# Two output tiles side by side, in alternating banks, in the loops of a two-layer decoder step's MLP

## The chip, the cores and the metric

The kernel runs on one core of a Trainium2 chip. The metric is the device time of one execution in microseconds (us); smaller is better. TensorE does the matrix products, VectorE (DVE), ScalarE (ACT) and GpSimd (POOL) the elementwise work, SyncE (SP) issues transfers. PSUM is the memory that TensorE writes to; the kernel sees it as 8 banks of 128 partitions x 512 fp32 numbers.

## The reference

One inference step of a two-layer decoder trunk, for a prompt of 1024 tokens and a sample group of 8 sequences x 8 tokens, which share all weights. Layer 0 mixes by sliding-window attention and a gated short convolution, layer 1 by multi-scale pooling and dilated attention. Each layer then is

```
x = layer_norm(ALPHA * x + mixer(x))
x = layer_norm(ALPHA * x + square(relu(x @ w1)) @ w2)     # the MLP: w1 is 1024 x 4096, w2 is 4096 x 1024
```

all in fp32, with D_MODEL = 1024. The change is in the second line alone. The caches of keys and values are also copied to new outputs, shifted by the 8 new tokens.

## The kernel before

**Layout.** Activations are kept with features on the partitions: X is [128, 8, 1088], that is 8 chunks (KC) of 128 features by 1024 + 64 tokens. The tokens are worked in three groups (GROUP) of 384, 384 and 320 columns.

**Products in three passes.** Each fp32 operand is split into a high part of type fp32r and the rest, also fp32r: XS (or HID) holds both for the activations, WS both for the weights. For each chunk k of the contraction there are three matmuls, high x high, low weight x high and high weight x low, all into the same bank. `product` (L1187 to L1195) writes such a unit: 3 x 8 = 24 matmuls of 128x128 weights by 384 (or 320) columns for an input product, 3 x 4 = 12 for a down product. Every matmul has a weight load of its own.

**The MLP.** The hidden width of 4096 is cut into N_HB = 8 blocks of 512. For each block the *hidden* stage (`hidden_super`) makes 12 units: for each group g, 4 tiles j of 128 hidden features, from weight tile j. The *down* stage (`down_super`) makes 24 units: for each group, 8 output tiles m, two (mm) from each of 4 weight tiles. The first hidden stage and the last down stage of a layer also carry the layer norm's transposes between their units (`weave` is not None, `ln_weave`); what lies between runs in a hardware loop of N_HB - 1 = 7 rounds per layer, each one down stage and one hidden stage, with `weave` None. TensorE's instructions run in program order, and so do those of each other engine; semaphores tie them together.

**Banks.** Hidden unit u writes bank 4 + u % 2, down unit v bank 6 + v % 2. Before a unit TensorE waits until the unit two before it has been taken out of the bank: `h_evac` (L1378 to L1380) or `p_evac` (L1396).

**Behind a hidden unit.** ScalarE waits for h_mm and makes Relu from the bank to RT (L621), Square to ST (L625), Copy to HID's high part (L627), then issues one part of the caches' copy (L641); VectorE subtracts to get HID's rest (L976, hid_ready). In the last group it then casts a weight tile of the down stage (L798, `w_high_loop`).

**Behind a down unit.** VectorE adds the bank to X (L995). In the last group it casts a tile of the next hidden stage after every second unit (L798).

**Weight tiles.** A tile is 128 x 1024. SyncE loads it into one of NRAW = 2 buffers WR (L316) as soon as the tile two before has been split; VectorE casts it to the high part in one of NSLOT = 4 slots of WS; GpSimd makes the rest (L458) and counts w_split, for which TensorE waits in group 0 of a stage. The cast stands in VectorE's program behind the work on the unit that last used that slot, and no semaphore other than that order guards the slot.

Of the kernel before, what the change touches and what calls it, by code (L numbers as in the profile page):

```python
# [12 lines left out]
P = 128  # L13
# [3 lines left out]
KC = D_MODEL // P  # L17
# [15 lines left out]
GROUP = ((0, 384), (384, 384), (768, 320))  # L33
# [11 lines left out]
NSLOT = 4  # L45
# [16 lines left out]
U_MLP = (U_EOUT + 3 * EVEN_OUT, U_EOUT + 3 * EVEN_OUT + N_HB * 24 + 3 * ODD_IN + 12 + 3 * ODD_OUT)  # L62
# [21 lines left out]
def build(nc, io):  # L84
    F32, F32R = mybir.dt.float32, mybir.dt.float32r
    ALU, ACT, AX = mybir.AluOpType, mybir.ActivationFunctionType, mybir.AxisListType
    ctx = ExitStack()
    with ctx:
        place = [nc.sbuf_base + (-nc.sbuf_base) % 64]

        def at(name, shape, dtype, offset):
            return nc.alloc_sbuf_tensor_at(name, shape, dtype, offset=offset)
# [17 lines left out]
        X = at("X", [P, KC, NT], F32, o_xr)  # L110
        XS = at("XS", [P, 2, KC, NT], F32R, o_xs)
        HID = at("HID", [P, 2, 4, NT], F32R, o_hr)
        Y = at("Y", [P, KC, NT], F32, o_hr)
        WS = at("WS", [P, NSLOT, 2, 1024], F32R, o_ws)
# [3 lines left out]
        RT = at("RT", [P, 2, 384], F32, o_scr + 12288)  # L118
# [77 lines left out]
        def bank(b, n=512):  # L196
            return PS[:, b, 0:n]

        def sem(name):
            return ctx.enter_context(nc.semaphore(name))  # L200
# [9 lines left out]
        p_mm, p_evac = sem("p_mm"), sem("p_evac")  # L210
        h_mm, h_evac, h_sq, hid_hi, hid_ready = sem("h_mm"), sem("h_evac"), sem("h_sq"), sem("hid_hi"), sem("hid_ready")
# [17 lines left out]
        def back_bank(l, g, k):  # L229

            return (2, 3, 6, 7)[k % 4] if (l, g) == (3, 2) else 2 + k % 2

        def rows_out(l, g):

            return ZE if (l, g) == (3, 2) else ZN
# [41 lines left out]
        def parts_d(m):  # L277

            n = 2 * (step_d(m)[1] + 1)
            return [(i, min(4, n - i)) for i in range(0, n, 4)]  # L280
# [6 lines left out]
        for m in range(STEPS_D + 2):  # L287
            b, phase = divmod(m, PER_SEQ)
# [214 lines left out]
        def _(act):  # L503
# [110 lines left out]
            def hidden_super(l, i, weave, copy):  # L614

                for g, (c0, gw) in enumerate(GROUP):
                    for j in range(4):
                        u = 4 * g + j
                        n = 12 * i + (H_UNITS * l + u)
                        act.wait_ge(h_mm, n + 1)  # L620
                        act.activation(RT[:, u % 2, 0:gw], bank(4 + u % 2, gw), ACT.Relu).then_inc(h_evac, 1)  # L621
                        act.wait_ge(h_evac, n + 1)
                        if not (isinstance(n, int) and n < 2):
                            act.wait_ge(hid_ready, n - 1)
                        act.activation(ST[:, u % 2, 0:gw], RT[:, u % 2, 0:gw], ACT.Square).then_inc(h_sq, 1)  # L625
                        act.wait_ge(h_sq, n + 1)
                        act.activation(HID[:, 0, j, c0:c0 + gw], ST[:, u % 2, 0:gw], ACT.Copy).then_inc(hid_hi, 1)  # L627
                        cache_copy(*copy, u)
                        if weave is not None and g < 2:
                            ln_weave(weave, 3 + g, j)  # L630

            def cache_copy(name, out, b, part):

                n = (D_WINDOW - DEC_SEQ) // COPY_PARTS
                if isinstance(b, int):
                    src, dst = io[name][b:b + 1], io[out][b:b + 1]
                else:
                    src, dst = io[name][bass.ds(b, 1)], io[out][bass.ds(b, 1)]
                src = src[:, DEC_SEQ + n * part:DEC_SEQ + n * (part + 1), :].rearrange("a s f -> a (s f)")
                dst = dst[:, n * part:n * (part + 1), :].rearrange("a s f -> a (s f)")  # L640
                act.dma_start(dst.rearrange("a (k f) -> (a k) f", k=16),  # L641
                              src.rearrange("a (k f) -> (a k) f", k=16)).then_inc(copied, 16)
# [90 lines left out]
            for m in range(STEPS_D):  # L733
                b, phase = divmod(m, PER_SEQ)
                n = len(parts_d(m))
# [32 lines left out]
        def _(dve):  # L768
# [26 lines left out]
            def w_high_loop(i, t):  # L795

                dve.wait_ge(w_in[t % NRAW], 64 * i + 16 * (t // NRAW + 1))
                dve.tensor_copy(WS[:, t % NSLOT, 0, :], WR[:, t % NRAW, :]).then_inc(w_hi, 1)  # L798
# [24 lines left out]
            def taken(u):  # L823
                return bank(6 + u % 2)
# [96 lines left out]
            for s in range(4):  # L921
                for g in range(3):
                    for j in range(4):
                        u = 12 * s + 4 * g + j
# [18 lines left out]
            for g in range(3):  # L943
                for j in range(2):
                    u = 48 + 2 * g + j
# [40 lines left out]
            def down_super(l, i, weave, first=False):  # L986
                for g, (c0, gw) in enumerate(GROUP):
                    for m in range(8):
                        v = 8 * g + m
                        dve.wait_ge(p_mm, 24 * i + (U_MLP[l] + v + 1))  # L990
                        if first:
                            dve.scalar_tensor_tensor(out=X[:, m, c0:c0 + gw], in0=X[:, m, c0:c0 + gw], scalar=ALPHA,  # L992
                                                     in1=taken(v)[:, 0:gw], op0=ALU.mult, op1=ALU.add).then_inc(p_evac, 1)
                        else:
                            dve.tensor_tensor(X[:, m, c0:c0 + gw], X[:, m, c0:c0 + gw], taken(v)[:, 0:gw],  # L995
                                              ALU.add).then_inc(p_evac, 1)
                        if g == 2 and m % 2 == 1:
                            if weave is None:
                                w_high_loop(i, T_MLP[l] + m // 2 + 2 * NSLOT)
                            elif l == 0:  # L1000
                                w_high(T_OIN + m // 2)
                        if weave is not None and m % 2 == 1:
                            ln_weave(weave, g, m // 2)
# [151 lines left out]
            for m in range(STEPS_D):  # L1155
                b, phase = divmod(m, PER_SEQ)
# [21 lines left out]
            c0, gw = GROUP[2]  # L1178
# [7 lines left out]
        def _(pe):  # L1186
            def product(out, slot, off, nk, src, g, done):  # L1187
# [7 lines left out]
                        n += 1  # L1195
                last.then_inc(done, 1)

            def unit(u, t, g):

                if g == 0:  # L1200
                    pe.wait_ge(w_split, t + 1)
                if u >= 2:
                    pe.wait_ge(p_evac, u - 1)
                product(bank(6 + u % 2), t % NSLOT, 0, KC, XS, g, p_mm)
# [161 lines left out]
            def hidden_super(l, i, weave, done):  # L1366

                t0 = T_MLP[l]
                for g in range(3):
                    if weave is not None:  # L1370
                        pe.wait_ge(x_split, XS_LN[2 * l] + 8 * (g + 1))
                        if g == 0:
                            pe.wait_ge(zn_ready, 18 * l + 5)
                    for j in range(4):
                        u = 4 * g + j
                        n = 12 * i + (H_UNITS * l + u)
                        if g == 0:
                            pe.wait_ge(w_split, 8 * i + (t0 + j + 1))  # L1378
                        if not (isinstance(n, int) and n < 2):
                            pe.wait_ge(h_evac, n - 1)  # L1380
                        product(bank(4 + u % 2), (t0 + j) % NSLOT, 0, KC, XS, g, h_mm)
                        if weave is not None and g < 2:
                            ln_weave(weave, 3 + g, j, done)

            def down_super(l, i, weave):

                t0 = T_MLP[l] + 4
                done = [U_MLP[l] + 24 * (N_HB - 1) + 8 * g + 8 for g in range(3)]
                for g in range(3):
                    pe.wait_ge(hid_ready, 12 * i + (H_UNITS * l + 4 * g + 4))  # L1390
                    for j in range(4):
                        if g == 0:
                            pe.wait_ge(w_split, 8 * i + (t0 + j + 1))
                        for mm in range(2):
                            v = 8 * g + 2 * j + mm
                            pe.wait_ge(p_evac, 24 * i + (U_MLP[l] + v - 1))  # L1396
                            product(bank(6 + v % 2), (t0 + j) % NSLOT, 4 * mm, 4, HID, g, p_mm)
                        if weave is not None:
                            ln_weave(weave, g, j, done)
                return done  # L1400
# [8 lines left out]
            done = mlp(0, out_projection(0, T_EOUT, U_EOUT, XS_MIX0))  # L1409
# [10 lines left out]
            for s in range(4):  # L1420
                for g in range(3):
                    if s == 0:
                        pe.wait_ge(x_split, XS_LN1 + 8 * (g + 1))
                    for j in range(4):
                        n = 4 * g + j
# [12 lines left out]
                if s == 2:  # L1438
# [3 lines left out]
                    for c in range(4):  # L1442
                        last = pe.transpose(PS[0:NS, 3, c * P:c * P + P], KTD[:, c, SEQ:NT], IDN[:, :])
# [97 lines left out]
            for m in range(STEPS_D):  # L1541
                b, phase = divmod(m, PER_SEQ)
                n = len(parts_d(m))
# [22 lines left out]
            done = mlp(1, out_projection(1, T_OOUT, U_OOUT, XS_MIX1))  # L1566
# [152 lines left out]
```

## Time and profile before

| what | us |
|---|---|
| median of 3 runs | 2589.13 |
| lowest and highest | 2588.72, 2597.13 |
| the profiled execution's own time | 2585.44 |
| its span, first to last instruction | 2583.4 |
| TensorE busy with matmuls in the span | 2462.0 |
| VectorE, ScalarE, GpSimd busy | 915.0, 627.0, 504.9 |

A profile is of one execution. Its groups name the source line, the engine, the operation and the tiles written and read; a group's busy time is the union of its instructions on the engine, so for overlapping matmuls it is less than count x mean: one matmul is in flight for 334 ns, while the next starts long before that. The step from one matmul to the next therefore has to be read from starts, not from the mean of one.

### The profile page before, as it was taken

How to read it: one execution, taken by the hardware profiler on the slowest of the kernel's cores; microseconds unless marked ns; L12 is line 12 of the kernel's file. 1: busy time of each engine (PE TensorE's matmuls, PEld its weight loads, DVE VectorE, ACT ScalarE, POOL GpSimd, SP SyncE). 2: the span in 40 equal slices, each digit the busy share in tenths (PEclk: the TensorE clock that was granted, in tenths of full speed). 3: DMA queues.
4: the chain of work that ended last, by engine and by line, in shares of the span. 5: the costliest groups of instructions: out<-in, count | busy, mean ns of one | idle time of the engine just before them, and what ended most of it. 6: DMA issues, size and time to landing. Idle time of an engine off the chain costs nothing.

```text
span 2583.4 us, 39454 instructions
## 1 busy us (share of the span) xinstructions
PE 2462.0 (95%) x16054; PEld 2344.8 (91%) x16054; DVE 915.0 (35%) x2028; ACT 627.0 (24%) x1352; POOL 504.9 (20%) x254
## 2 busy tenths in 40 slices
PE   6999998999999999998999798898999999999996
PEld 6988997999999999998998455798999999999995
DVE  3455534222322322327135445434322322322325
ACT  1223305121121022023101556505121121122122
POOL 2111214221211211213220000114221211211210
PEclk9999999999999999999999899999999999999998
DMA  5200412232232232222111956402232232232221
GB/s 161 72 22 32 119 33 66 74 122 65 81 113 70 84 105 76 92 92 82 54 58 59 274 191 250 143 33 66 78 118 70 80 109 76 87 97 81 87 76 70
DMA packets 77253, 240.12 MB, mean 93 GB/s; under 512 B 25168, under 2 KB 42192, under 8 KB 69328
## 3 DMA queue, kind: packets, MB, share of 16 engines
q1 hardware_dynamic: 60464, 167.65, 19.4%
q10 hardware_dynamic: 16688, 71.05, 9.5%
q8 instruction: 73, 1.20, 0.2%
q14 instruction: 28, 0.23, 0.0%
HBM read 224.78 MB, written 81.71 MB: 119 GB/s over the span
## 4 chain that ended last, share of the span: by engine, by line
PE 80%; issue 7%; DVE 6%; ACT 3%; POOL 2%; DMA 1%; SPq 1%; POOLq 0%; DVEq 0%; ACTq 0%
PE PS L1193 70%; POOL WS L458 2%; PE PS L1222 1%; PE PS L1471 1%; PE PS L1457 1%; DVE ZN L820 1%; PE PS L1483 1%; PE PS L1496 1%; PE PS L1522 1%; PE PS L1271 1%; PE PS L1238 1%; DMA KC<-in_kt 1%; DVE XS L785 1%; ACT X L539 1%; DMA WR<-in_w 1%
## 5 line engine op out<-in xcount | busy, mean ns | idle before, releaser
L1193 PE MATMUL PS<-XS,WS 128*128 128x384 f32 (+1 forms) x8208 | 1382.9, 328 | 33.8 <-DVE XS L785 19.5
L1193 PEld LDWEIGHTS PS<-XS,WS 128*128 128x128 f32 x8208 | 1355.5, 189 | 48.5 <-issue 36.1
L458 POOL TENSOR_TENSOR WS<-WR,WS 128x1024 fp32r<-128x1024 f32 x178 | 436.1, 2450 | 1900.2 <-DVE WS L798 1059.9
L1193 PE MATMUL PS<-HID,WS 128*128 128x384 f32 (+1 forms) x4608 | 765.4, 326 | 2.2 <-DVE X L995 2.1
L1193 PEld LDWEIGHTS PS<-HID,WS 128*128 128x128 f32 x4608 | 758.3, 188 | 4.6 <-DVE X L995 4.3
L621 ACT ACTIVATE RT<-PS 128x384 f32<-128x384 f32 (+1 forms) x192 | 91.0, 474 | 1113.3 <-PE PS L1193 1113.3
L976 DVE TENSOR_TENSOR HID<-ST,HID 128x384 fp32r<-128x384 f32 (+1 forms) x192 | 105.8, 551 | 632.2 <-ACT HID L627 632.2
L995 DVE TENSOR_TENSOR X<-X,PS 128x384 f32<-128x384 f32 (+1 forms) x336 | 177.5, 531 | 401.3 <-PE PS L1193 401.1
L625 ACT ACTIVATE ST<-RT 128x384 f32<-128x384 f32 (+1 forms) x192 | 97.5, 508 | 7.8
L627 ACT ACTIVATE HID<-ST 128x384 fp32r<-128x384 f32 (+1 forms) x192 | 97.5, 508 | 6.1
L471 POOL TENSOR_TENSOR XS<-X,XS 128x384 fp32r<-128x384 f32 (+1 forms) x72 | 69.0, 967 | 91.7 <-ACT XS L543 88.1
L798 DVE CAST WS<-WR 128x1024 fp32r<-128x1024 f32 x112 | 77.0, 688 | 9.7 <-DMA WR<-in_w 9.2
L539 ACT ACTIVATE X<-PS,COLS 128x384 f32<-128x384 f32 (+1 forms) x92 | 59.0, 647 | 56.8 <-PE PS L1222 55.9
L548 ACT ACTIVATE SD<-VE 128x1 f32<-128x1 f32 (+1 forms) x36 | 7.3, 203 | 255.9 <-DVE VE L810 255.9
L962 DVE TENSOR_TENSOR X<-X,PS 128x384 f32<-128x384 f32 (+1 forms) x48 | 25.3, 529 | 114.6 <-PE PS L1193 114.3
L1222 PE MATMUL PS<-IDN,ZN 128*128 128x128 f32 (+1 forms) x264 | 44.5, 288 | 21.7 <-ACT X L539 13.2
L1222 PEld LDWEIGHTS PS<-IDN,ZN 128*128 128x128 f32 (+1 forms) x264 | 31.0, 144 | 34.7 <-ACT X L539 19.2
L793 DVE CAST WS<-WR 128x1024 fp32r<-128x1024 f32 x66 | 49.5, 751 | 12.5 <-DMA WR<-in_w 12.3
L820 DVE TENSOR_SCALAR ZN<-PS,MV,RS 128x1024 f32<-128x1024 f32 (+1 forms) x33 | 44.3, 1343 | 10.9 <-PE PS L1222 9.9
L992 DVE SCALAR_TENSOR_TENSOR X<-X,PS 128x384 f32<-128x384 f32 (+1 forms) x48 | 25.5, 531 | 60.7 <-PE PS L1193 60.7
L1457 PE MATMUL PS<-KTD,Y 64*128 64x512 f32 (+3 forms) x192 | 43.6, 554 | 1.6 <-DVE MNA L1110 0.7
L1471 PEld LDWEIGHTS PS<-IDN,SMB 128*128 128x128 f32 x208 | 26.3, 160 | 18.1 <-DVE SMB L1122 10.6
(166 smaller groups left out, 1220.4 us busy)
## 6 DMA issues: line engine op xcount, KB each, us to landing
WR<-in_w SPq DMA_DIRECT2D x178, 512.0 KB, 3.3
out_d_ks<-in_cache_d_k ACTq DMA_DIRECT2D x96, 340.0 KB
out_d_vs<-in_cache_d_v ACTq DMA_DIRECT2D x96, 340.0 KB
KC<-in_kt SPq DMA_DIRECT2D x16, 1024.0 KB, 9.7
VCD<-in_cache_d_v SPq DMA_DIRECT2D x16, 1024.0 KB, 7.2
TH<-in_th SPq DMA_DIRECT2D x4, 1024.0 KB, 8.2
KC<-in_kt SPq DMA_DIRECT2D x8, 512.0 KB, 6.5
VCD<-in_cache_d_v SPq DMA_DIRECT2D x32, 128.0 KB, 7.4
```

What stands on the lines that cost most here:

```text
L458: pool.tensor_tensor(WS[:, slot, 1, :], WR[:, raw, :], WS[:, slot, 0, :].bitcast(F32), ALU.subtract).then_inc(w_split, 1)
L539: act.activation(X[:, k, c0:c0 + gw], bank(back_bank(l, g, k), gw), ACT.Identity, scale=col(C_LNG + KC * l + k), bias=col(C_LNB + KC * l + ...
L621: act.activation(RT[:, u % 2, 0:gw], bank(4 + u % 2, gw), ACT.Relu).then_inc(h_evac, 1)
L625: act.activation(ST[:, u % 2, 0:gw], RT[:, u % 2, 0:gw], ACT.Square).then_inc(h_sq, 1)
L627: act.activation(HID[:, 0, j, c0:c0 + gw], ST[:, u % 2, 0:gw], ACT.Copy).then_inc(hid_hi, 1)
L798: dve.tensor_copy(WS[:, t % NSLOT, 0, :], WR[:, t % NRAW, :]).then_inc(w_hi, 1)
L820: dve.tensor_scalar(rows_out(l, g)[0:r, tt, :], FT[0:r, :], MV[0:r, 0:1], RS[0:r, 0:1], ALU.subtract, ALU.mult).then_inc(zn_ready, 1)
L976: dve.tensor_tensor(HID[:, 1, j, c0:c0 + gw], ST[:, u % 2, 0:gw], HID[:, 0, j, c0:c0 + gw].bitcast(F32), ALU.subtract).then_inc(hid_ready, 1)
L995: dve.tensor_tensor(X[:, m, c0:c0 + gw], X[:, m, c0:c0 + gw], taken(v)[:, 0:gw], ALU.add).then_inc(p_evac, 1)
L1193: last = pe.matmul(out[:, 0:gw], WS[:, slot, a, (off + k) * P:(off + k + 1) * P], src[:, b, k, c0:c0 + gw], start=(n == 0), stop=(n == 3 * ...
L1222: last = pe.transpose(PS[:, back_bank(l, g, k), tt * P:tt * P + r], rows_out(l, g)[0:r, tt, k * P:k * P + P], IDN[0:r, 0:r])
L1457: last = pe.matmul(bank(2 * (u % 2) + h, nk * P), Y[rows, 4 + c, qb * P:qb * P + P], KTD[rows, c, k * P:(k + nk) * P], start=True, stop=True)
```

## The change

In the loops alone (`weave` None), two units are issued together: `pair` goes through the 24 (hidden) or 12 (down) steps, and at each makes one matmul for the first output tile and one for the second, in two banks. A hidden pair is units u - 1 and u, of two weight tiles; a down pair is the two output tiles v and v + 1 of one weight tile. Four banks serve each kind: hidden pairs take 4, 5 and 0, 1 by turns, down pairs 6, 7 and 2, 3. A pair waits once, until the pair before the last is out of its banks. The counters h_mm and p_mm are raised at the last matmul of each tile, which are now the last two of a pair. The readers on ScalarE and VectorE look into the new banks, in the same order as before; the woven stages are as they were.

```diff
+        def hidden_bank(u, paired):
+            return (4, 5, 0, 1)[u % 4] if paired else 4 + u % 2
+        def down_bank(v, paired):
+            return (6, 7, 2, 3)[v % 4] if paired else 6 + v % 2
...
-                        act.activation(RT[:, u % 2, 0:gw], bank(4 + u % 2, gw), ACT.Relu).then_inc(h_evac, 1)
+                        act.activation(RT[:, u % 2, 0:gw], bank(hidden_bank(u, weave is None), gw), ACT.Relu).then_inc(h_evac, 1)
...
-                            dve.tensor_tensor(X[:, m, c0:c0 + gw], X[:, m, c0:c0 + gw], taken(v)[:, 0:gw],
+                            dve.tensor_tensor(X[:, m, c0:c0 + gw], X[:, m, c0:c0 + gw], bank(down_bank(v, weave is None), gw),
                                               ALU.add).then_inc(p_evac, 1)
...
+            def pair(outs, weights, nk, src, g, done):
+                c0, gw = GROUP[g]
+                n = 0
+                for k in range(nk):
+                    for a, b in ((0, 0), (1, 0), (0, 1)):
+                        for out, (slot, off) in zip(outs, weights):
+                            last = pe.matmul(out[:, 0:gw], WS[:, slot, a, (off + k) * P:(off + k + 1) * P],
+                                             src[:, b, k, c0:c0 + gw], start=(n == 0), stop=(n == 3 * nk - 1))
+                            if n == 3 * nk - 1:
+                                last.then_inc(done, 1)
+                        n += 1
...
+                        if weave is None:
+                            if j % 2:
+                                pe.wait_ge(h_evac, n - 1 if u == 1 else n - 3)
+                                pair((bank(hidden_bank(u - 1, True)), bank(hidden_bank(u, True))),
+                                     (((t0 + j - 1) % NSLOT, 0), ((t0 + j) % NSLOT, 0)), KC, XS, g, h_mm)
+                            continue
...
+                        if weave is None:
+                            v = 8 * g + 2 * j
+                            pe.wait_ge(p_evac, 24 * i + (U_MLP[l] + (v if v == 0 else v - 2)))
+                            pair((bank(down_bank(v, True)), bank(down_bank(v + 1, True))),
+                                 (((t0 + j) % NSLOT, 0), ((t0 + j) % NSLOT, 4)), 4, HID, g, p_mm)
+                            continue
```

TensorE at the start of a down stage in the loop, before (REGISTER_ALU and ISA rows compute or make a wait against a counter of the loop):

```order
L1393 ISA [waits hid_ready]
L1396 ISA [waits w_split]
L1193 MATMUL PS<-HID,WS 128x384 [waits p_evac]
L1193 MATMUL PS<-HID,WS 128x384 x11
L1396 REGISTER_ALU
L1193 MATMUL PS<-HID,WS 128x384 [waits p_evac]
L1193 MATMUL PS<-HID,WS 128x384 x11
L1393 REGISTER_ALU
L1396 REGISTER_ALU [waits w_split]
```

and of the changed kernel at the same place:

```order
L1420 ISA [waits hid_ready]
L1423 ISA [waits w_split]
L1213 MATMUL PS<-HID,WS 128x384 [waits p_evac]
L1213 MATMUL PS<-HID,WS 128x384 x23
L1420 REGISTER_ALU
L1213 MATMUL PS<-HID,WS 128x384 [waits p_evac,w_split]
L1213 MATMUL PS<-HID,WS 128x384 x23
```

Two runs of 12 matmuls, each behind a wait for its bank, have become one run of 24 behind one wait. The waits for weight tiles stand where they stood, one for every 24 matmuls.

TensorE at the start of a hidden stage in the loop, before:

```order
L1378 ISA
L1380 ISA [waits w_split]
L1193 MATMUL PS<-XS,WS 128x384 [waits h_evac]
L1193 MATMUL PS<-XS,WS 128x384 x23
L1378 REGISTER_ALU
L1193 MATMUL PS<-XS,WS 128x384 [waits h_evac,w_split]
L1193 MATMUL PS<-XS,WS 128x384 x23
```

and of the changed kernel:

```order
L1399 ISA
L1399 REGISTER_ALU [waits w_split]
L1402 REGISTER_ALU [waits w_split]
L1213 MATMUL PS<-XS,WS 128x384 [waits h_evac]
L1213 MATMUL PS<-XS,WS 128x384 x47
```

Here the wait for the second weight tile has moved ahead of the first unit's matmuls: the stage starts when two tiles are split, and 48 matmuls follow one wait.

## Rows read from the trace of the kernel before

**Rows 1.** The page: busy us of TensorE, its granted clock in tenths, the two dearest matmul groups.

```profile
PE 2462.0 (95%) x16054; PEld 2344.8 (91%) x16054; DVE 915.0 (35%) x2028; ACT 627.0 (24%) x1352; POOL 504.9 (20%) x254
...
PEclk9999999999999999999999899999999999999998
...
L1193 PE MATMUL PS<-XS,WS 128*128 128x384 f32 (+1 forms) x8208 | 1382.9, 328 | 33.8 <-DVE XS L785 19.5
...
L1193 PE MATMUL PS<-HID,WS 128*128 128x384 f32 (+1 forms) x4608 | 765.4, 326 | 2.2 <-DVE X L995 2.1
```

**Rows 2.** Stretches (from:to, us, busy by engine, clock): both loops, a down half, a hidden half.

```profile
472.01:1135.33 663.32, 663.19 (x4029) 662.41 (x4028) 170.52 (x308) 125.21 (x252) 134.48 (x56) 1.00 0.28 88
1827.00:2490.00 663.00, 662.97 (x4027) 662.15 (x4026) 168.96 (x308) 125.18 (x252) 133.64 (x56) 1.00 0.27 88
...
899.24:946.62 47.38, 47.38 (x291) 47.38 (x289) 8.94 (x16) 16.51 (x33) 7.98 (x5) 1.00 0.36 114
851.69:899.24 47.55, 47.55 (x291) 47.34 (x289) 15.23 (x28) 1.38 (x3) 11.23 (x5) 1.00 0.19 62
```

**Rows 3.** Timeline of TensorE: start, us to the last end, group [idle before, releaser].

```profile
851.69 47.71 PE L1193 MATMUL PS<-HID,WS 128*128 128x384 f32 x288
899.24 47.54 PE L1193 MATMUL PS<-XS,WS 128*128 128x384 f32 x288
```

**Rows 4.** Timeline of ScalarE, the Relus of units that follow each other.

```profile
907.78 0.49 ACT L621 ACTIVATE RT<-PS 128x384 f32<-128x384 f32 x1 [2.47 <-PE PS L1193]
...
911.94 0.49 ACT L621 ACTIVATE RT<-PS 128x384 f32<-128x384 f32 x1 [2.55 <-PE PS L1193]
...
936.26 0.44 ACT L621 ACTIVATE RT<-PS 128x320 f32<-128x320 f32 x1 [1.91 <-PE PS L1193]
...
939.78 0.44 ACT L621 ACTIVATE RT<-PS 128x320 f32<-128x320 f32 x1 [2.08 <-PE PS L1193]
```

**Rows 5.** Timeline of TensorE, two matmuls each: within a unit, across units, at a stage's start.

```profile
908.63 0.51 PE L1193 MATMUL PS<-XS,WS 128*128 128x384 f32 x2
...
907.41 0.51 PE L1193 MATMUL PS<-XS,WS 128*128 128x384 f32 x2
...
899.41 0.52 PE L1193 MATMUL PS<-XS,WS 128*128 128x384 f32 x2
```

**Rows 6.** Timeline of VectorE, the evacuations of two down units that follow each other.

```profile
858.33 0.56 DVE L995 TENSOR_TENSOR X<-X,PS 128x384 f32<-128x384 f32 x1 [1.69 <-PE PS L1193]
860.40 0.55 DVE L995 TENSOR_TENSOR X<-X,PS 128x384 f32<-128x384 f32 x1 [1.52 <-PE PS L1193]
```

**Rows 7.** Timeline of TensorE: first down matmuls of each loop and behind each loop.

```profile
472.01 0.51 PE L1193 MATMUL PS<-HID,WS 128*128 128x384 f32 x2
...
1136.14 0.51 PE L1193 MATMUL PS<-HID,WS 128*128 128x384 f32 x2
...
1826.80 3.48 PE L1193 MATMUL PS<-HID,WS 128*128 128x384 f32 x19
...
2490.88 1.40 PE L1193 MATMUL PS<-HID,WS 128*128 128x384 f32 x7
```

**Rows 8.** Timeline around the longest wait for a bank, 658 to 668 us.

```profile
657.55 2.41 POOL L458 TENSOR_TENSOR WS<-WR,WS 128x1024 fp32r<-128x1024 f32 x1 [1.11 <-DVE WS L798]
...
663.67 3.52 PE L1193 MATMUL PS<-HID,WS 128*128 128x384 f32 x17
...
665.01 0.69 DVE L798 CAST WS<-WR 128x1024 fp32r<-128x1024 f32 x1 [0.91 <-DMA WR<-in_w]
665.62 1.06 DVE L995 TENSOR_TENSOR X<-X,PS 128x384 f32<-128x384 f32 x2
```

**Rows 9.** Timeline behind the second unit of a hidden stage's last group.

```profile
844.85 0.44 ACT L621 ACTIVATE RT<-PS 128x320 f32<-128x320 f32 x1 [2.08 <-PE PS L1193]
...
846.33 0.49 DVE L976 TENSOR_TENSOR HID<-ST,HID 128x320 fp32r<-128x320 f32 x1 [2.43 <-ACT HID L627]
...
846.73 0.69 DVE L798 CAST WS<-WR 128x1024 fp32r<-128x1024 f32 x1
847.50 2.41 POOL L458 TENSOR_TENSOR WS<-WR,WS 128x1024 fp32r<-128x1024 f32 x1 [1.11 <-DVE WS L798]
```

More of the change, by code:

```diff
@@ L992, in down_super @@
                             dve.scalar_tensor_tensor(out=X[:, m, c0:c0 + gw], in0=X[:, m, c0:c0 + gw], scalar=ALPHA,
-                                                     in1=taken(v)[:, 0:gw], op0=ALU.mult, op1=ALU.add).then_inc(p_evac, 1)
+                                                     in1=bank(down_bank(v, weave is None), gw), op0=ALU.mult, op1=ALU.add).then_inc(p_evac, 1)
                         else:
-                            dve.tensor_tensor(X[:, m, c0:c0 + gw], X[:, m, c0:c0 + gw], taken(v)[:, 0:gw],
+                            dve.tensor_tensor(X[:, m, c0:c0 + gw], X[:, m, c0:c0 + gw], bank(down_bank(v, weave is None), gw),
                                               ALU.add).then_inc(p_evac, 1)
```

## The prediction

> **What bounds the kernel now.** I read the page first. Its busy table gives TensorE 2462.0 of 2583.4 us at a granted clock of nine tenths or more nearly everywhere, and the dearest groups are the three-pass products of L1193 [rows 1]. So the question is not which engine bounds the MLP's loops, but whether TensorE waits in them or what one of its steps costs. The table by stretches answers the first half: over the two loops TensorE is busy 663.19 of 663.32 us and 662.97 of 663.00 us, at a clock of 1.00 (the 2.4 GHz level), while VectorE has 170 us of work, ScalarE 125, GpSimd 134 [rows 2]. In the timeline one hidden half of 288 products starts at 899.24 and the next down half at 946.62, 47.38 us later; the down half before it began at 851.69 and took 47.55 [rows 2, 3].
>
> The second half is the step. Successive Relus of a hidden stage start 4.16 us apart for 384 columns and 3.52 us apart for 320 [rows 4]; a unit is 24 matmuls, so a step is 173.3 ns and 146.7 ns. The 64 columns between them cost 26.7 ns, 0.417 ns each (one column per cycle at 2.4 GHz). So 384 columns stream for 160.0 ns and every step carries a fixed 13.3 ns that does not depend on the columns. Check: 192 x 173.3 + 96 x 146.7 = 47.36 us, against 47.38 measured. The hidden half has nothing in it but steps.
>
> **The change part by part.** The loops make 2 layers x 7 rounds x 576 = 8064 of the matmuls. Their number, sizes and weight loads stay; only their order does not.
>
> *Banks alternate at every matmul.* In the kernel before, the bank changes once per unit. The trace has that case: two matmuls within a unit (908.63 on) fill 0.51 us from the first start to the last end; the last of one unit and the first of the next, which writes the other bank (907.41 on), fill 0.51 us too [rows 5]. The unit's own period says it more finely: 23 steps inside at 173.3 ns leave 4.16 - 3.986 = 0.174 us for the one that changes banks. Down units: 2.07 us for 12 steps, 172.5 ns within the rounding, with a bank change twice as often and no dearer [rows 6]. So a bank change is neither gain nor loss, and I take 0 for it. What the rows do not show is a matmul that adds to a bank other than the one just written; the first of a unit overwrites. Bounds: at best the whole 13.3 ns goes, 8064 x 13.3 ns = 107 us; at worst each step becomes like the longest step without a wait, 12 ns more (two matmuls in 0.52 us rather than 0.51; I read the extra as 5 to 15 ns) [rows 5], 8064 x 12 ns = 97 us. Both ends are far; the nearest row is the bank change itself, at zero.
>
> *Fewer waits for a free bank.* The pair waits for banks that were left a whole pair earlier. In the loops this replaces waits that are nearly all over already. What they cost now is measured from loop start to loop end: 472.01 to 1136.14 is 664.13 us, 1826.80 to 2490.88 is 664.08 us [rows 7]; fourteen rounds without a stall would be 14 x 2 x 47.38 = 1326.64 (a down half has the same columns and steps), so 1.57 us are lost in all. Where: just behind a hidden stage VectorE has to cast the fourth weight tile, whose transfer is late (idle 0.91 us on the DMA), and the first evacuation of the down stage stands behind it in VectorE's program; TensorE's third unit waits for that bank. In the worst case 17 matmuls take 3.52 us where 16 x 173.3 + 334 ns = 3.11 was due, 0.41 us lost [rows 8]. With four banks the third unit needs no old bank; the evacuation is first needed by the third pair, 8.3 us into the stage. The stall goes: 1.57 us gained.
>
> *Later evacuation of the even unit.* Both units of a pair end together, so the even one is taken 4.16 us later in a hidden stage (2.08 in a down stage). ScalarE needs 1.48 us from a Relu's start to the end of HID's Copy [rows 9], twice that and two transfer issues, 3 to 3.6 us, per pair of 7.0 to 8.3 us; VectorE 1.1 us (two of 0.55 [rows 6]) per down pair of 4.2: hidden.
>
> *Weight tiles.* These follow the evacuations. Take the down stage that starts at 851.69 [rows 3]. The four units of the 320-column group ahead of it end 3.52 us apart [rows 4], the second at 844.85 and the fourth at 851.89; after, they end as pairs at these two times. The rows show what follows a unit that ends at 844.85: its Relu then, VectorE's rest at 846.33, the cast at 846.73, GpSimd's rest at 847.50 for 2.41 us [rows 9]. So down tile 0 takes exactly the time that tile 1 has now: ready at 849.91, needed at 851.69, 1.8 us to spare. Tile 1 is cast meanwhile and leaves GpSimd at 849.91 + 2.4 = 852.3; the second down pair needs it one pair of 4.16 us in, at 855.85. Tile 2 may be loaded from 849.91; the longest time from release to cast is 665.01 - (657.55 + 2.41) = 5.05 us [rows 8], so cast at 854.96, ready 858.1, needed at 860.0: 1.9 to spare. Tile 3: loaded from 852.3, cast 857.4, ready 860.6, needed at 864.2. VectorE takes pair 0 of the down stage behind that cast, 858.0 to 859.1; pair 2 wants the banks at 860.0: 0.9 us to spare, the smallest margin of all. The other way round (tiles of the next hidden stage, cast in the down stage's last group) the cast moves by one evacuation, 0.49 us. A hidden pair needs both its tiles at its start: tiles 0 and 1 at once, 2 and 3 8.3 us later. Down pairs of 320 columns end 3.52 us apart, the last at the stage's start; two evacuations, the cast of 0.69 and GpSimd's 2.41 us end some 4.1 us behind a pair. So tile 1 is ready 7.04 - 4.1 = 2.9 us before the stage begins and tile 3 4.1 us after. Hidden, at no cost.
>
> The Trainium skill, trace analysis page (Perfetto Trace Analysis, section "Matmul Optimizations"), asks that all 8 PSUM banks be used for more parallelism; by that rule this change should pay. The trace bounds what it can be worth here at the 1.57 us above, since TensorE has no other wait in the loops. The page TensorE: Matmul & The Clock Gate (section "Back-to-back issue gap") gives a warm gap of N/2.4 + 2.5 ns, against the fixed 13.3 ns here. By it some 10.8 ns of each step would be avoidable, an estimate of 87 us if the alternation avoided it; its gap is for an isolated stream, and this trace has no step as short.
>
> **Sum.** Profiled execution: span 2583.4 - 1.6 = 2581.8, its time 2585.44 - 1.6 = 2583.9. The median of the three runs is 3.7 us above the profiled one; the forecast keeps that: 2589.13 - 1.6 = 2587.5 us, rounded.
>
> **The rivals.** (A) The fixed 13.3 ns is a wait of an accumulation on its own bank, and alternation hides it. For it: it is independent of the column count, and back-to-back adds to one bank is what the change breaks up. Against: the step that changes banks is as long. 2589.1 - 107 - 2 = 2480 us; half of it, 2534. 5%.
> (B) Slower: the weight transfer at the hidden-to-down seam. Now ScalarE issues its cache copies a unit apart (3.52 us); after, two within 2 us right behind each pair, just where tiles 2 and 3 are loaded. Place: the cast of tile 3 holds VectorE, pair 2 of the down stage waits. It begins to cost when release to cast passes 5.05 + 0.9 = 6.0 us; it makes the kernel over 0.3% slower once 14 seams cost (7.8 + 1.6) / 14 = 0.67 us each, thus from 6.7 us on; at double the longest now seen, 10.1 us, it costs 14 x 4.1 = 57 us, 2645 us. For it: the longest is 5.05 us already, and it made VectorE idle [rows 8]. Against: that much more has no row. 5%.
> (C) Adding to the other bank costs a little, as bounded above: up to 97 us, 2685; over 0.3% from (7.8 + 1.6) us / 8064 = 1.2 ns a step. Against: the same row as for A. 3%.
> (D) The change doesn't do what it says: were the pairs reordered back or serialised, the time would be 2587 to 2589 as well; no separate chance.
>
> **How the numbers follow.** 0.3% is 7.8 us, about what a measurement of this kernel tells from no change. My forecast (step unchanged, stall gone, nothing else late) has 87%, and its own spread is that of the runs before, 2588.72 to 2597.13, and of a few us of seams: 2580 to 2597, all within the 0.3% but for the last 2%. Faster 0.07 (A and 2 for its weaker forms and the runs' scatter), slower 0.09 (B, C and scatter), same 0.84. The rivals' times are so far off and so rare that the range leaves them out: 2578 to 2598.
>
> **What would show it.** Right: hidden halves of 47.38 us, down halves all 47.38 and none longer, Relus in twos, 8.32 us apart, the step 173.3 ns, the two loops 663.3 us each, the cast of down tile 0 some 3.5 us later. Wrong: any step other than 173 ns in the pairs (A or C), TensorE waiting on the cast or on X's evacuation 8 us into a down stage (B), a wait for w_split at the first pair.

## The result, and the profile after

The change makes the kernel a little slower. Over 12 runs each its median is 2596.74 us (2592.64 to 2601.79) against 2589.07 us (2583.07 to 2597.85); the ratio is 1.0025, 95% interval 1.0014 to 1.0036, that is 3.6 to 9.3 us more. The forecast was 2587.5 us and no change that a measurement can tell. One of the 11 executions of the kernel before that the first four experiments stand beside took 6184.87 us; every ratio is of the other, fast ones.

The first thing to look at is what the forecast rested on: the loops. The timeline of TensorE in the changed kernel (start, us to the last end, group, count) and a stretch of 200 us (from:to, us, busy us of TensorE, its weight loads, VectorE, ScalarE, GpSimd, then the granted clock):

```profile
573.44 47.54 PE L1213 MATMUL PS<-HID,WS 128*128 128x384 f32 x288
620.82 0.51 PE L1213 MATMUL PS<-XS,WS 128*128 128x384 f32 x2
```

```profile
600.00:800.00 200.00, 200.00 (x1218) 200.00 (x1218) 53.03 (x93) 35.75 (x72) 38.77 (x16) 1.00 0.27 84
```

A down half lasts from 573.44 to 620.82, 47.38 us, what a half without a stall took before [rows 2, 3]; of the 28 halves in the two loops' 14 rounds, 25 read 47.38 and the others 47.41. TensorE is busy without a gap, and the Relus of a hidden stage come in twos, 8.32 us apart. So alternation costs and gives nothing per step, and the 1.57 us of small stalls [rows 7] are all but gone. Both parts came out as forecast. The page shows where something did change:

```profile
L984 DVE TENSOR_TENSOR HID<-ST,HID 128x384 fp32r<-128x384 f32 (+1 forms) x192 | 145.7, 759 | 631.5 <-ACT HID L635 631.2
...
L1201 PE MATMUL PS<-HID,WS 128*128 128x384 f32 (+1 forms) x576 | 101.7, 335 | 8.3 <-DVE X L1003 8.3
```

The second row is the woven down stages, the ones behind the loops, which the change did not touch: TensorE idles 8.3 us before them, waiting for VectorE's addition to X. Before, all the down stages together had 2.2 us of that [rows 1]. The first row says that VectorE's subtraction for HID's rest now takes 759 ns in the mean; the page of the kernel before has 551 ns for it (its L976): 25 of the 192 take over 1 us, where 2 did.

The timeline at the first of the two places, behind the loop of layer 0, unfolds it:

```profile
1137.70 2.40 POOL L466 TENSOR_TENSOR WS<-WR,WS 128x1024 fp32r<-128x1024 f32 x1 [39.02 <-DVE WS L806]
...
1138.34 2.11 DVE L984 TENSOR_TENSOR HID<-ST,HID 128x320 fp32r<-128x320 f32 x1 [0.72 <-ACT HID L635]
...
1142.04 4.35 PE L1201 MATMUL PS<-HID,WS 128*128 128x384 f32 x24
...
1144.52 0.69 DVE L806 CAST WS<-WR 128x1024 fp32r<-128x1024 f32 x1 [0.46 <-DMA WR<-in_w]
...
1145.29 2.36 POOL L466 TENSOR_TENSOR WS<-WR,WS 128x1024 fp32r<-128x1024 f32 x1 [1.76 <-DVE WS L806]
1145.42 2.58 DVE L984 TENSOR_TENSOR HID<-ST,HID 128x320 fp32r<-128x320 f32 x1 [0.20 <-ACT HID L635]
1148.07 0.69 DVE L806 CAST WS<-WR 128x1024 fp32r<-128x1024 f32 x1
1148.67 1.01 DVE L1003 TENSOR_TENSOR X<-X,PS 128x384 f32<-128x384 f32 x2
...
1149.37 6.84 PE L1201 MATMUL PS<-HID,WS 128*128 128x384 f32 x29 [2.98 <-DVE X L1003]
```

TensorE makes two units (24 matmuls) from 1142.04 and then wants bank 6 back for the third. VectorE is still at the work of the last hidden pair: a subtraction that takes 2.58 us because GpSimd's split runs beside it, the fourth cast, and only then the addition that frees the bank. The third unit starts at 1149.37 instead of 1146.22, 3.15 us late; at the second place it is 3.41 us, and there it is the load of the fourth tile that comes last: VectorE was idle for 0.86 us, until its transfer had landed, ahead of the cast at 2508.17. And it does not end there. The stretch behind the wait:

```profile
1151.00:1154.00 3.00, 3.00 (x11) 3.00 (x10) 0.55 (x1) 0.00 (x0) 0.22 (x1) 0.50 0.50 175
```

The granted clock is 0.50, the 1.2 GHz level, after TensorE had stood still for 3 us; eleven matmuls are in flight in 3 us, a step of 320 ns. Summed over the steps that are too long, about ten at each place, this adds 1.6 us at each. The account: 2 x (3.3 + 1.6) = 9.8 us lost, 1.6 us gained, 8.2 us, against 7.7 us between the medians.

The profiled execution of the changed kernel has a span of 2599.8 us, 16.4 us over before, not 8.2. The other 8 us lie outside: its first loop alone starts at 478.68 against 472.01 [rows 7]. Nothing was changed ahead of that loop. The clock differs there: in the changed kernel's trace it is 0.50 in the stretches 270.5 to 273.3, 410.5 to 413.3, 444.5 to 447.3 and 454.8 to 457.6 us, and 1.00 at the same places of the trace before. The kernel with four banks and no pairs, below, whose time is that of before, has the clock at 0.50 in the same four stretches and its first loop at 478.55. So these 6.7 us don't come with the change; why one execution loses the clock there and another doesn't is open.

### The profile page after: what moved, and what is told of

Same layout as the page of the kernel before. It is cut to its first block, busy times and chain, and to the rows that moved or that the text cites. A ratio compares the mean times of both kernels' runs of the same rounds, so it can differ in the third digit from the quotient of the medians.

```text
span 2599.8 us, 39202 instructions
## 1 busy us (share of the span) xinstructions
PE 2470.7 (95%) x16054; PEld 2354.9 (91%) x16054; DVE 939.9 (36%) x2028; ACT 627.0 (24%) x1352; POOL 505.7 (19%) x254
## 4 chain that ended last, share of the span: by engine, by line
PE 87%; DVE 6%; ACT 3%; DMA 1%; SPq 1%; issue 1%; POOL 1%; ACTq 0%; DVEq 0%
PE PS L1213 50%; PE PS L1201 27%; PE PS L1243 1%; PE PS L1504 1%; PE PS L1490 1%; DVE ZN L828 1%; PE PS L1516 1%; DMA WR<-in_w 1%; PE PS L1529 1%; PE PS L1259 1%; PE PS L1555 1%; PE PS L1292 1%; DMA KC<-in_kt 1%; DVE XS L793 1%; ACT X L547 1%
## 5 line engine op out<-in xcount | busy, mean ns | idle before, releaser
L984 DVE TENSOR_TENSOR HID<-ST,HID 128x384 fp32r<-128x384 f32 (+1 forms) x192 | 145.7, 759 | 631.5 <-ACT HID L635 631.2
L1003 DVE TENSOR_TENSOR X<-X,PS 128x384 f32<-128x384 f32 (+1 forms) x336 | 164.6, 528 | 378.3 <-PE PS L1213 335.9
L970 DVE TENSOR_TENSOR X<-X,PS 128x384 f32<-128x384 f32 (+1 forms) x48 | 25.4, 530 | 114.6 <-PE PS L1201 114.3
L1243 PEld LDWEIGHTS PS<-IDN,ZN 128*128 128x128 f32 (+1 forms) x264 | 31.5, 145 | 34.9 <-ACT X L547 19.5
```

What stands on the lines that cost most here:

```text
L984: dve.tensor_tensor(HID[:, 1, j, c0:c0 + gw], ST[:, u % 2, 0:gw], HID[:, 0, j, c0:c0 + gw].bitcast(F32), ALU.subtract).then_inc(hid_ready, 1)
L1243: last = pe.transpose(PS[:, back_bank(l, g, k), tt * P:tt * P + r], rows_out(l, g)[0:r, tt, k * P:k * P + P], IDN[0:r, 0:r])
```

## The experiments

### Four banks in the woven down stage

```diff
-            return (6, 7, 2, 3)[v % 4] if paired else 6 + v % 2
+            return (6, 7, 2, 3)[v % 4] if paired or v < 8 else 6 + v % 2
...
-                            pe.wait_ge(p_evac, 24 * i + (U_MLP[l] + v - 1))
-                            product(bank(6 + v % 2), (t0 + j) % NSLOT, 4 * mm, 4, HID, g, p_mm)
+                            pe.wait_ge(p_evac, 24 * i + (U_MLP[l] + (v - 3 if v < 8 else v - 1)))
+                            product(bank(down_bank(v, False)), (t0 + j) % NSLOT, 4 * mm, 4, HID, g, p_mm)
```

> The changed kernel, and in the last down stage of each layer (the one outside the loop, which follows a paired hidden stage) the first token group's eight units use banks 6, 7, 2, 3 in turn and wait for the bank four units back. Theory 1 (seam): the loss is TensorE's wait for bank 6 at the third unit of that stage, 3.15 and 3.4 us in the profile, and the half-clock steps behind it, some 1.4 us each: 2 x 4.7 = 9.4 us come back, so 2596.7 - 9.4 = 2587.3 us, ratio to before 0.9993. Rival 2 (step): the alternation of banks costs something spread over the loops, which this edit leaves: 2596 us. Rival 3 (drift ahead of the loops, 6.7 us later at the first loop in the one profile): 2590 to 2596 us, with the profile's first loop again starting some us later than at 472 us.

Measured: 2586.16 us, beside 2589.36 for the kernel before on the same chip; ratio 0.9988 (0.9973 to 1.0002). The whole loss is gone with two places of the program edited. The step is out as the cause, and so is a drift of the size that rival 3 needs (2590 us at least; the interval ends at 2589.9). The timeline of TensorE at the place, now without a gap:

```profile
1138.12 8.16 PE L1201 MATMUL PS<-HID,WS 128*128 128x384 f32 x46
```

46 matmuls in 8.16 us, (8.16 - 0.33) / 45 = 174 ns a step. VectorE is as late as in the changed kernel (its first addition starts 6.82 us into the stage, there 6.63); the third unit no longer asks. By the two ratios, 1.0014 at least and 1.0002 at most, this version beats the changed kernel, though the two were not run side by side; against the kernel before, the interval just holds no change.

### Only the down stages paired

The changed kernel without the branch for pairs in `hidden_super`, and with `bank(4 + u % 2, gw)` in ScalarE's Relu.

> Only the down stages of the loops are paired (banks 6, 7, 2, 3); hidden units are made one by one in banks 4, 5 as before. Theory 1 (seam): the wait needs a paired hidden stage ahead of a two-bank down stage, and there is none, so the time is that of before less the 1.6 us of small stalls in the loops: 2587.5 us; third unit of the woven down stage waits at most 0.4 us. Rival 2 (step): down pairs are a third of a hidden and down round's... half of the loops' matmuls, so half of the loss stays: 2593 us.

Measured: 2585.26 us; ratio 0.9987 (0.9968 to 1.0005). With alternating banks in half of the loops' matmuls nothing is lost: it is the hidden pairs that bring the wait. One point of the expectation missed: at the second place the third unit waits 0.66 us, not 0.4 at most (0.00 at the first). There VectorE was idle for 1.37 us ahead of the fourth cast, until the load had landed: the small stall of the kernel before, with a later load.

### Only the hidden stages paired

The changed kernel without the branch for pairs in `down_super`, and with `taken(v)` in VectorE's additions.

> Only the hidden stages of the loops are paired; all down stages, in the loops too, are made unit by unit in two banks. Theory 1 (seam): now each of the 14 paired hidden stages is followed by a two-bank down stage, whose third unit waits some 3.2 us for bank 6 and then runs about 1.4 us longer at half the clock: 14 x 4.6 = 64 us over before, 2653 us; without the clock's part 2634 us. The down halves in the loops read 50.6 to 52 us. Rival 2 (step): 2593 us, nothing special at the seams.

Measured: 2662.42 us; ratio 1.0282 (1.0263 to 1.0301), 73 us over before. Now every paired hidden stage has a two-bank down stage behind it, and the cost repeats: in its profile there are 14 waits of 2.9 to 3.7 us at these seams, one of 1.06 us at the first down stage of layer 0 (whose hidden stage is not paired), together 46.9 us, and 27.2 us of steps that are too long behind them, 74.1 in all. The forecast was 9 us short: the long steps cost 1.4 to 2.9 us at a seam, not 1.4, and the down halves behind a paired hidden stage take 51.8 to 53.7 us. One seam in the timeline:

```profile
670.37 4.35 PE L1201 MATMUL PS<-HID,WS 128*128 128x384 f32 x24
...
673.08 2.38 POOL L466 TENSOR_TENSOR WS<-WR,WS 128x1024 fp32r<-128x1024 f32 x1 [1.21 <-DVE WS L806]
...
673.72 2.08 DVE L984 TENSOR_TENSOR HID<-ST,HID 128x320 fp32r<-128x320 f32 x1 [0.72 <-ACT HID L635]
676.77 0.69 DVE L806 CAST WS<-WR 128x1024 fp32r<-128x1024 f32 x1 [0.97 <-DMA WR<-in_w]
677.38 1.01 DVE L1003 TENSOR_TENSOR X<-X,PS 128x384 f32<-128x384 f32 x2
```

Nearly the same picture: 2.08 us of subtraction until just behind GpSimd's end, then 0.97 us for the load of the tile, then the cast, then the bank.

### Four banks, no pairs

```diff
-                            if j % 2:
-                                pe.wait_ge(h_evac, n - 1 if u == 1 else n - 3)
-                                pair(...)
+                            pe.wait_ge(h_evac, n - u if u < 4 else n - 3)
+                            product(bank(hidden_bank(u, True)), (t0 + j) % NSLOT, 0, KC, XS, g, h_mm)
                             continue
...
+                            for mm in range(2):
+                                v = 8 * g + 2 * j + mm
+                                pe.wait_ge(p_evac, 24 * i + (U_MLP[l] + (0 if v < 4 else v - 3)))
+                                product(bank(down_bank(v, True)), (t0 + j) % NSLOT, 4 * mm, 4, HID, g, p_mm)
```

> The loops' units use the four banks in turn, as in the changed kernel, but are made one after the other, no pairs. Theory 1 (seam): evacuations and casts keep the pace of before, so no seam wait; the four banks remove the small stalls of the loops: 2587.5 us, down halves all 47.38 us. Rival 2 (the new banks themselves, 0 to 3, cost something, wherever): 2593 to 2597 us.

Measured: 2587.97 us; ratio 0.9997 (0.9982 to 1.0012), and down halves in the loops of 47.38 us. The interval ends at 2592.5 us, below rival 2: the banks themselves are neutral. The small stalls go, but 1.6 us is below what these runs resolve.

### What makes VectorE so late: four edits on the kernel with hidden pairs only

That kernel shows the seam 14 times, so a part of a wait can be measured there.

(a) Square in PSUM, so that the subtraction reads one tile of SBUF instead of two:

```diff
+                        sq = bank(2 + u % 2, gw) if weave is None else ST[:, u % 2, 0:gw]
-                        act.activation(ST[:, u % 2, 0:gw], RT[:, u % 2, 0:gw], ACT.Square).then_inc(h_sq, 1)
+                        act.activation(sq, RT[:, u % 2, 0:gw], ACT.Square).then_inc(h_sq, 1)
```

and `sq` as the source of HID's Copy and of VectorE's subtraction.

> As the kernel with hidden pairs only (2662 us, seam waits of 2.9 to 3.7 us, mean 3.3), but in the loops ScalarE puts the Square into the free banks 2 and 3 of PSUM instead of ST, so VectorE's subtraction for HID's rest has one operand in SBUF instead of two. Theory A (shared port): that subtraction takes 2.1 to 2.6 us where it meets GpSimd's split only because both read two tiles in SBUF; now none of the loops' takes over 0.7 us. The second cast then starts some 1.5 us earlier, the tile's split ends 1.0 us earlier (behind GpSimd's first), and with it the load and the fourth cast: waits 3.3 - 1.0 = 2.3 us, 14 of them, 14 us less, 2648 us. Rival B (GpSimd slows any VectorE instruction, whatever its operands): subtractions and waits stay, 2662 us.

(b) GpSimd splits 512 of a tile's 1024 columns in the loops and leaves the rest of the other 512 uncomputed:

```diff
-                pool.tensor_tensor(WS[:, slot, 1, :], WR[:, raw, :], WS[:, slot, 0, :].bitcast(F32),
+                pool.tensor_tensor(WS[:, slot, 1, 0:w], WR[:, raw, 0:w], WS[:, slot, 0, 0:w].bitcast(F32),
```

> As the kernel with hidden pairs only, but in the loops GpSimd splits the first 512 of a weight tile's 1024 columns and leaves the rest part of the others as it was (part of the computation is left out). GpSimd's instruction takes 1.2 us instead of 2.4. Theory A (the chain cast, split, load, cast, evacuation sets the wait, and the subtraction is held by the split): held subtractions end 1.2 us sooner, loads are released 1.2 to 2.2 us sooner, waits 1.5 to 1.8 us instead of 3.3; 2662 - 14 x 1.7 = 2638 us, less if the clock then stays up. Rival B (the wait is TensorE's for something else than VectorE's evacuation): 3.3 us stay.

(c) Half of each tile is loaded in the loops; the other half keeps old numbers:

```diff
-                sp.dma_start(WR[:, (t0 + j) % NRAW, :],
-                             io["w"][bass.ds(t, 1), :, :].rearrange("a p n -> (a p) n")).then_inc(w_in[(t0 + j) % NRAW], 16)
+                sp.dma_start(WR[:, (t0 + j) % NRAW, 0:512],
+                             io["w"][bass.ds(t, 1), :, 0:512].rearrange("a p n -> (a p) n")).then_inc(w_in[(t0 + j) % NRAW], 16)
```

> As the kernel with hidden pairs only, but the loops load only the first 512 columns of each weight tile (the others keep old numbers; part of the computation is left out). From a tile's release to its cast then takes some 3 us instead of 4.5. Theory A (fourth cast waits for both, the held subtraction and the load, about equally late): the subtraction still ends at 5.6 to 5.9 us into the stage, so the waits shrink only by 0.3 to 0.6 us, to 2.8: 2655 us. Rival C (the load alone sets it): waits 3.3 - 1.5 = 1.8 us, 2641 us.

(d) Both (a) and (c).

> Both edits: the Square in PSUM and half weight loads, on the kernel with hidden pairs only. Theory A: neither the subtraction nor the load holds the fourth cast; it starts about 4.0 us into the stage and the first evacuation ends at 5.1: waits of 1.1 us, what the pairs' late end alone costs, since ScalarE's second unit and VectorE's work for it only end 3.9 us into the stage. 2662 - 14 x 2.2 = 2631 us, and to 2606 us if a wait this short leaves the clock up. Rival C: as with half loads alone.

Measured, with the waits for the bank and the excess of the steps that are too long behind them, each summed over the 16 down stages of one profile; the usual wait is the median of the down stages behind a hidden pair:

| kernel | us | ratio to before | waits, us: sum, usual one | long steps, us |
|---|---|---|---|---|
| hidden pairs only | 2662.42 | 1.0282 (1.0263 to 1.0301) | 46.9, 3.3 | 27.2 |
| (a) Square in PSUM | 2634.58 | 1.0169 (1.0126 to 1.0213) | 34.9, 2.3 (1.9 to 3.3) | 12.1 |
| (b) half split | 2615.22 | 1.0098 (1.0064 to 1.0133) | 22.6, 1.27 | 4.3 |
| (c) half load | 2643.80 | 1.0198 (1.0171 to 1.0226) | 35.6, 2.37 | 21.1 |
| (d) (a) and (c) | 2612.36 | 1.0090 (1.0061 to 1.0120) | 28.4, 1.89 | 1.4 |

The first row was measured beside a kernel before of 2589.36 us, the others on another chip beside one of 2591.25 us. The two last columns account for the time over before to within 9 us. The two down stages behind the loops have waits of 2.3 to 3.7 us in all four; their own weight tiles are loaded and split outside the loop, in full in (b) and (c) too.

(a) The time is 28 us less rather than 14 (four runs, 2623 to 2645 us), because the waits were followed by the half clock less often (12.1 us against 27.2). VectorE's rows on its page:

```profile
L985 DVE TENSOR_TENSOR HID<-PS,HID 128x384 fp32r<-128x384 f32 (+1 forms) x168 | 89.9, 535 | 560.1 <-ACT HID L636 559.7
...
L807 DVE CAST WS<-WR 128x1024 fp32r<-128x1024 f32 x112 | 100.9, 901 | 20.1 <-DMA WR<-in_w 20.1
```

The subtraction takes 535 ns in the mean, against 784 with two operands in SBUF; of 192 one takes over 1 us, against 28, and that one is of a stage with ST. So it is not GpSimd's work as such that holds the subtraction, but where its operands lie. But the hold did not go away, it moved to the cast: 901 ns in the mean against 687, and 23 of the 112 over 1 us, where none was. The second cast at a seam now begins beside GpSimd's first split and is held until behind its end (1.94 us from 670.09, where the split ends at 671.47), so the second split starts only 0.4 us earlier, counted from the first, and not 1.0 as theory A had it. That the usual wait came out at A's 2.3 us is in part luck; the single waits lie between 1.9 and 3.3, and in the longest VectorE was idle for 2.52 us ahead of the fourth cast, until the load had landed.

(b) saved more than expected: the wait is 1.27 us rather than 1.5 to 1.8, and behind it the clock stayed up. Half of the 47 us saved is waits, half is the clock. It shortens the hold and releases the loads earlier at once, and doesn't say which counts for how much.

(c) fell between A's 2.8 and C's 1.8. The fourth cast no longer waits for the load but follows the held subtraction at once, and is 1 us earlier for it: both set the fourth cast, neither alone.

(d) missed: 1.89 instead of 1.1 us. Its timeline shows why:

```profile
669.32 2.37 POOL L466 TENSOR_TENSOR WS<-WR,WS 128x1024 fp32r<-128x1024 f32 x1 [1.59 <-DVE WS L807]
...
669.94 0.49 DVE L985 TENSOR_TENSOR HID<-PS,HID 128x320 fp32r<-128x320 f32 x1 [0.70 <-ACT HID L636]
670.70 1.54 DVE L807 CAST WS<-WR 128x1024 fp32r<-128x1024 f32 x1 [0.27 <-DMA WR<-in_w]
672.16 1.00 DVE L1004 TENSOR_TENSOR X<-X,PS 128x384 f32<-128x384 f32 x2
```

The subtraction is free (0.49 us beside GpSimd), and the cast, SBUF to SBUF, meets GpSimd's split: 1.54 us instead of 0.69. I had counted it at 0.69. Its long steps, 1.4 us in all, are one step of 0.1 us too much behind each wait; the clock never left the 2.4 GHz level at a seam.

## Why the prediction was wrong

- *Step unchanged*: right. 47.38 us per half in the changed kernel, and per down half and hidden half in each variant where nothing is waited for; rivals A and C did not occur.
- *Small stalls removed*: right in kind; 1.5 of the 1.57 us went.
- *Weight tiles hidden in the loops*: right. No wait for w_split or for a bank in the loops, although the margin of 0.9 us for pair 2 was worked out without a held subtraction: the second unit's takes 2.1 us where it meets the split, not 0.49.
- *Later evacuation of the even unit* and *Weight tiles*, put at "hidden" and "at no cost" for the seams behind the loops too: this is the step that failed. The working asked who waits for VectorE in the down stage that follows, and answered with four banks: "the evacuation is first needed by the third pair, 8.3 us into the stage". That holds for the paired down stages. The last hidden stage of each loop is paired too, and the down stage behind it is the woven one, with two banks, where the third unit needs the first evacuation 4.17 us in. The prediction's own numbers already price it: VectorE done with pair 0's first addition at 858.6 by the worst load, needed at 851.69 + 4.17 = 855.86, so 2.7 us twice. The front matter's "the woven stages are as they were" was true of their code and not of what reaches them.
- *Its size*: 3.15 and 3.41 us rather than 2.7, although the loads took 4.4 and 4.8 us from release to cast and not the 5.05 reckoned: a held subtraction stands in the chain. The trace of before had the sign of it, which the prediction doesn't mention:

```profile
661.36 2.40 POOL L458 TENSOR_TENSOR WS<-WR,WS 128x1024 fp32r<-128x1024 f32 x1 [1.41 <-DVE WS L798]
663.42 0.69 DVE L976 TENSOR_TENSOR HID<-ST,HID 128x320 fp32r<-128x320 f32 x1 [2.13 <-ACT HID L627]
```

  The subtraction ends 0.35 us behind GpSimd's end of 663.76. Before, the casts came a unit apart and the subtraction nearly always missed the split (7 of 192 took over 0.6 us); two units at once put the second unit's subtraction right onto the first tile's split.
- *The clock* has no term in the prediction. Its fall behind each wait cost 1.6 us. With it the seams cost 2 x (3.3 + 1.6) = 9.8 us where the prediction had nothing.
- Rival B had the right place in VectorE's program (the fourth cast, the seam) but the wrong partner: it looked for 14 seams with a slow load, and gave 5%. It was two seams, and no load slower than the 5.05 us seen before was needed.
- The signs that were to show the forecast right came true, for they were all of the loops, where it is right. And the measured 2596.74 us lies in the range of 2578 to 2598 by luck: the range was made for the scatter of runs and a few us of seams, not for this loss.

## What to carry to other kernels

When a stage in a loop is given more buffers, list every consumer and follower of it, and above all the peeled first and last stages: they keep the old depth but get the new rhythm. Finishing two tiles together saves nothing for a TensorE that is always busy and bunches everything behind it; the work of the second tile then overlaps what the first one set off, here GpSimd's split. Where the engine that is waited for is VectorE, check which of its instructions overlap GpSimd's, and where their operands lie.

## What the runs showed of the hardware

- A VectorE subtraction with both operands in SBUF, started while GpSimd works on SBUF tiles, ends some 0.35 us behind GpSimd's instruction, whatever is left of it (2.11 us from 1138.34, GpSimd's end 1140.10; 2.58 us from 1145.42, its end 1147.65; alone 0.49). In the changed kernel all 25 that started with over 0.3 us of GpSimd's work left did so. With one operand in PSUM it takes 0.49 us beside GpSimd, 24 times of 24 in (a) and 27 of 27 in (d). A cast from SBUF to SBUF is held in the same way, and ends some 0.55 us behind GpSimd's instruction (1.54 or 1.94 us instead of 0.69); the additions to X, one operand in PSUM, are not held (0.55 us each). In all of these GpSimd had started first; for the other order nothing is shown here.
- The Trainium skill, page SBUF — State Buffer, section "Who interferes with whom", says so: a VectorE instruction with two SBUF inputs contends with a GpSimd instruction that reads SBUF, and a cast can run in a two-port mode that contends too; the shared ports go to the one that issues first for its whole instruction, and the other blocks fully. The numbers above agree; in which mode the cast ran, no run here shows.
- By that rule a held subtraction could have been priced before the run, from rows of the kernel before; this is an estimate. The first tile's split starts 1.17 us behind the first unit's subtraction (847.50 - 846.33) and takes 2.41 [rows 9]; the second unit's subtraction comes 1.5 to 1.8 us behind the first (the prediction's 3 to 3.6 us of ScalarE's work for a pair). Held until 0.35 us behind the split's end, it takes 2.1 to 2.4 us instead of 0.49, 1.6 to 1.9 us more. Measured at 1138.34: 2.11 us.
- A gap of 3 us in TensorE's work was mostly followed by a loss at the 1.2 GHz level, usually of some 1.6 us: behind all 14 waits over 2.9 us of the kernel with hidden pairs only (1.4 to 2.9 us each), but not behind two of 3.15 and 3.29 us in (a) nor one of 3.25 us in (d). In (b), waits of 1.27 to 1.35 us left the clock at the 2.4 GHz level, 12 of 12; in (d) waits of 1.89 us did, 12 of 12, while in (a) one of 1.94 us did not, and in (c) it fell behind 10 of 12 waits of 2.4 us. So the length of the gap alone doesn't decide it.
- A matmul that adds to another bank than the one before it takes as long as one that adds to the same: 173.3 ns for 384 columns, 47.38 us for 288 matmuls, either way. What the fixed 13.3 ns beyond the streaming is was not tried.
